# Regrouping the end of a recurrence and the products around its group norm, in a two-layer decoder step

## The reference, cut to what matters

```python
def step(s, inp):                     # one token of the recurrence; s is the state of each head, 64 x 64
    r_t, w_t, k_t, v_t, kk_t, kka_t = inp
    sa = einsum('bhvk,bhk->bhv', s, -kk_t)
    s = s * w_t[:, :, None, :] + sa[..., None] * kka_t[:, :, None, :] + v_t[..., None] * k_t[:, :, None, :]
    return s, einsum('bhvk,bhk->bhv', s, r_t)
...
mu = mean(y, -1); var = mean(square(y - mu), -1)          # over each head's 64 channels
y = ((y - mu) * rsqrt(var + GN_EPS)) * lnx_g + lnx_b
y = (y + bonus) * g                                       # g: the gate, sigmoid(gd) @ gate_up
...
out = concat([ya, yb], -1) @ w_out                        # ya from the recurrence, yb from the gMLP gate
```

## Time and profile before

| | |
|---|---|
| median of 3 runs | 1141.65 us (1141.34 to 1144.91) |
| profiled execution: its own time | 1145.79 us |
| profiled execution: span, first to last instruction | 1144.0 us |
| mean granted TensorE clock in it | 0.961 of full |
| busy: TensorE matmul | 1076.3 us |
| busy: VectorE | 804.7 us |
| busy: ScalarE | 640.1 us |
| DMA | 271.07 MB, mean 237 GB/s |

### The profile page before, as it was taken

How to read it: one execution, slowest core, us unless ns; L and a number is a source line. 1 busy time by engine, 2 the same in 40 slices (tenths; PEclk the granted TensorE clock), 3 DMA queues, 4 the chain that set the end, 5 groups by cost and what they waited for, 6 DMA issues and landing times.

```text
span 1144.0 us, 17555 instructions
## 1 busy us (share of the span) xinstructions
PE 1076.3 (94%) x7410; PEld 899.2 (79%) x7410; DVE 804.7 (70%) x901; ACT 640.1 (56%) x652; POOL 16.2 (1%) x23
## 2 busy tenths in 40 slices
PE   8999999999999999999967988889999999999996
PEld 8999889877688888888856956568768888888884
DVE  5358545475778989989852676374578898988983
ACT  4556223433666777777742332464367777777672
POOL 0000000000000000000003000000000000000000
PEclk9989999699999999999987989989999999999998
DMA  9332100225479999999926478562458999999961
GB/s 345 122 112 81 39 3 3 75 100 200 185 287 355 351 351 351 361 358 350 359 90 249 148 272 313 204 254 97 162 216 312 353 350 346 361 360 357 357 241 48
DMA packets 40324, 271.07 MB, mean 237 GB/s; under 512 B 5056, under 2 KB 5520, under 8 KB 9520
## 3 DMA queue, kind: packets, MB, share of 16 engines
q1 hardware_dynamic: 39616, 267.11, 63.2%
q0 software_dynamic: 624, 2.76, 0.6%
HBM read 265.78 MB, written 4.07 MB: 236 GB/s over the span
## 4 chain that ended last, share of the span: by engine, by line
PE 84%; DVE 6%; ACT 3%; DMA 3%; issue 3%; SPq 0%; DVEq 0%; ACTq 0%
PE ps L908 10%; PE ps L909 10%; PE ps L910 10%; PE ps L934 5%; PE ps L936 5%; PE ps L935 5%; PE ps L355 4%; PE ps L356 4%; PE ps L357 4%; PE ps L1716 3%; DMA arena<-in_k_near 3%; PE ps L946 1%; PE ps L921 1%; PE ps L947 1%; ACT w_hi L340 1%
## 5 line engine op out<-in xcount | busy, mean ns | idle before, releaser
L347 DVE TENSOR_TENSOR w_lo<-raw,w_hi 128x2048 fp32r<-128x2048 f32 x76 | 174.0, 2289 | 46.8 <-ACT w_hi L340 46.8
L340 ACT ACTIVATE w_hi<-raw 128x2048 fp32r<-128x2048 f32 x76 | 145.4, 1914 | 93.8 <-PE ps L357 38.0
L347 DVE TENSOR_TENSOR lo_more<-raw_more,hi_more 128x2048 fp32r<-128x2048 f32 x48 | 109.9, 2289 | 20.6 <-ACT hi_more L340 20.6
L347 DVE TENSOR_TENSOR w_lo<-raw_more,w_hi 128x2048 fp32r<-128x2048 f32 x48 | 109.9, 2290 | 15.6 <-ACT w_hi L340 15.5
L347 DVE TENSOR_TENSOR lo_more<-raw,hi_more 128x2048 fp32r<-128x2048 f32 x48 | 109.9, 2290 | 15.3 <-ACT hi_more L340 15.3
L340 ACT ACTIVATE hi_more<-raw 128x2048 fp32r<-128x2048 f32 x48 | 91.9, 1915 | 27.6 <-PE ps L910 27.6
L355 PE MATMUL ps<-h_hi,w_hi 128*128 128x320 f32 x320 | 103.2, 323 | 0.0
L340 ACT ACTIVATE w_hi<-raw_more 128x2048 fp32r<-128x2048 f32 x48 | 92.0, 1917 | 16.8 <-PE ps L936 16.8
L356 PE MATMUL ps<-h_lo,w_hi 128*128 128x320 f32 x320 | 101.0, 316 | 0.0
L357 PE MATMUL ps<-h_hi,w_lo 128*128 128x320 f32 x320 | 100.6, 314 | 0.0
L340 ACT ACTIVATE hi_more<-raw_more 128x2048 fp32r<-128x2048 f32 x48 | 91.9, 1914 | 11.4 <-PE ps L936 10.0
(11 more groups left out here) (502 smaller groups left out, 2335.4 us busy)
## 6 DMA issues: line engine op xcount, KB each, us to landing
raw<-in_stream SPq DMA_DIRECT2D x125, 1024.0 KB, 7.0
raw_more<-in_stream SPq DMA_DIRECT2D x96, 1024.0 KB, 7.1
arena<-in_k_near SPq DMA_DIRECT2D x8, 1024.0 KB, 9.5
arena<-in_v_near SPq DMA_DIRECT2D x8, 1024.0 KB, 7.5
arena<-in_k_far SPq DMA_DIRECT2D x8, 512.0 KB, 5.2
arena<-in_v_far SPq DMA_DIRECT2D x8, 512.0 KB, 5.0
arena<-in_bias_prompt SPq DMA_DIRECT2D x1, 1536.0 KB, 7.7
xt<-in_x SPq DMA_DIRECT2D x2, 640.0 KB, 4.8
```

What stands on the lines that cost most here:

```text
L340: eng.activation(hi_slot(W_SLOT[c]), raw_chunk(c), ACT.Copy).then_inc(S("w_hi_made"), 1)
L347: eng.tensor_tensor(lo_slot(W_SLOT[c]), raw_chunk(c), hi_slot(W_SLOT[c]), ALU.subtract).then_inc(S("w_lo_made"), 1)
```

## The change

It moves work within the engines' lists and adds four filler matmuls; nothing is computed differently. On VectorE the sample chunk's `add(2, 2)` goes ahead of `step(3)`, and `split_lo(AT_OUT0)` goes behind `y_add(4, 2)`. On TensorE four fillers of 128x256 go between `chunk_rest(4, 2)` and the wait for `y_made`. The output products of row tiles 4 to 7 are regrouped: tiles 0 and 1 whole (24 matmuls) ahead of the sum of squares (18 before), tile 2 whole (12) between that and the spread (12 before, of tiles 1 and 2), and half of tile 3 (6) between the spread and the gate (12 before, of tiles 2 and 3). The six matmuls after the gate stay.

```diff
             wkv_pe(eng)
+            for _ in range(4):
+                eng.matmul(ps[:, 1, 256:512], h_hi[:, 0, 0:P], h_hi[:, 0, 0:256], start=True, stop=True)
             eng.wait_ge(S("y_made"), 5)
...
             out0_rows(eng, 0, (4, 5, 6, 7), True, False)
-            out0_rows(eng, 1, (4, 5), True, False)
+            out0_rows(eng, 1, (4, 5, 6, 7), True, False)
             eng.wait_ge(S("mix0_vector"), MIX0_VECTOR["gn_centred"])
             eng.wait_ge(S("gn_sq"), 1)
             head_sums(eng, 0, s5).then_inc(S("gn_sums"), 1)
-            out0_rows(eng, 1, (6, 7), False, False)
-            out0_rows(eng, 2, (4, 5), True, False)
+            out0_rows(eng, 2, (4, 5, 6, 7), True, False)
             eng.wait_ge(S("mix0_vector"), MIX0_VECTOR["gn_turned"])
             for j in range(HT):
                 head_spread(eng, j, j, gn_rinv).then_inc(S("gn_spread"), 1)
-            out0_rows(eng, 2, (6, 7), False, False)
             out0_rows(eng, 3, (4, 5), True, False)
...
             eng.tensor_tensor(gu, gu, sbias, ALU.mult).then_inc(S("mix0_vector"), 1)
+            add(2, 2)
             step(3)
-            add(2, 2)
             y_add(3)
...
             eng.tensor_tensor(out, add_, ps[0:TS, 0, :].rearrange("p (j w t) -> p w j t", j=HT, w=2), ALU.add).then_inc(S("rhs_made"), 1)
-            split_lo(eng, AT_OUT0)
             eng.wait_ge(S("q_done"), 5)
             eng.tensor_copy(SET_S.e2[0:TS].rearrange("p s t -> p (s t)"), ps[0:TS, 3, :]).then_inc(S("q_kept"), 1)
             eng.wait_ge(S("sample_as_kept"), 2)
             y_add(4, 2)
+            split_lo(eng, AT_OUT0)
```

## The result

| | before | after |
|---|---|---|
| median | 1141.3 us (1134.95 to 1147.26, 20 runs) | 1133.83 us (1129.6 to 1139.35, 20 runs) |
| ratio to before | | 0.9932, 95% interval 0.9914 to 0.9951 |
| profiled execution, span | 1144.0 us | 1133.0 us |
| mean granted clock of the profiled execution | 0.961 | 0.970 |

The change makes the kernel 7.5 us faster by the medians and 7.8 us by the ratio. The two profiled executions differ by more, 11.0 us of span; why is a question for the experiments.

The account below looks back on a forecast made before the run. TensorE, 84% of the chain that ended last, was taken to bound the kernel. 1145.79 - 8.9 - 1.1 = 1135.8 us against the profile, 1131.7 against the median, taken as 1132.8; range 1129.5 to 1140.5.

Parts of the forecast that it names:

- The gap and its cause: Ahead of `third(2)`: TensorE idles because `add(2, 2)` stands behind `step(3)` on VectorE; moving it wins 1.55 us.
- The clock as most of the gain: Up to the end of the head sums: 8.9 us won, 1.55 from the gap, the rest from full clock.
- step 4: Ahead of `chunk_solved`: `add(2, 3)` waits behind L2169 on VectorE, so `chunk_solved` starts some 0.15 us late.
- step 5: At the solution's copy: moving `split_lo(AT_OUT0)` is worth nothing at half clock, about 1 us at full clock.
- step 7: Ahead of the head sums: four new fillers in a 0.59 us gap cost nearly 0.1 us at full clock, 0.6 at half.
- The load behind the split: Load behind `split_lo(AT_OUT0)`: comes some 8 us later relative to TensorE's work, needed only far behind; costed at nothing.
- The regrouping: From the mean to `sample_adds`: net 0.5 us, with half the second low stretch 1.1 us, between 0.5 and 1.8.
- that term: Second low stretch, behind the squares' sum: 1.3 us more won if it goes; half was taken.
- The turns: Rival: the clock falls later, at the turns after `third(2)`; 1140.6 us against the profile, 1136.5 against the median; chance 0.16.
- My sum: Both stretches, from `add(2, 2)` to `sample_adds`: 8.9 and 1.1 us won, 1145.79 to 1135.8 us against the profile.
- the rival of the unprofiled executions: Rival: unprofiled executions had no such low stretch, so only 2.5 to 4 us gained, 1137.7 to 1139; chance 0.09.
- My allowance for executions without the long stretch: Whole time: a fast execution may already lack part of the low stretch, so 1132.8 us instead of 1131.7.

Follow-up runs that it names:

- experiment 1: Changed kernel with `add(2, 2)` put back behind `step(3)`, so the idle time ahead of `third(2)` returns: 1141.14 us, ratio 0.9998 to the kernel before.
- experiment 9: Changed kernel with `add(2, 2)` put back behind `step(3)` and nine fillers of 128x256 ahead of `third(2)`: 1131.98 us, ratio 0.9927 to the kernel before.
- experiment 2: Kernel before with only `add(2, 2)` moved ahead of `step(3)`: 1138.55 us, ratio 0.9976.
- experiment 6: Changed kernel with `split_lo(AT_OUT0)` put back in front of the solution's copy: 1138.56 us, ratio 0.9965 to the kernel before.
- experiment 5: Kernel before with nine fillers of 128x256 between `chunk_writes(3)` and `third(2)`, VectorE's order untouched: 1140.75 us, ratio 0.9990.
- experiment 3: Changed kernel without the four new fillers: 1132.96 us, ratio 0.9917 to the kernel before.
- execution 7: One more profiled execution of the kernel before, unchanged: 1139.40 us.
- execution 8: One more profiled execution of the changed kernel, unchanged: 1128.81 us.
- execution 11: A later profiled execution of the kernel before, unchanged: 1136.81 us.
- experiment 4: Changed kernel with the output products grouped as before (18, 12, 12 and 6 matmuls): 1134.52 us, ratio 0.9967 to the kernel before.

## Why the prediction was right

**The gap and its cause.** Right. L2089 starts as soon as the products of `second(2)` are there, and TensorE goes on from `chunk_writes(3)` to `third(2)` without a break.

**The clock as most of the gain.** Right, and shown: experiments 1 and 9 differ in nothing but whether TensorE idles ahead of `third(2)` or works on fillers, and their ratios differ by 0.7%, with `third(2)` starting 6.06 us behind `second(2)` in both. The chain from the start of `second(2)` to the mean was worked out as 14.8 us (196.05 to 210.85); it took 14.95 (198.08 to 213.03), with 8.7 us won against my 8.9. The small wait of step 4 is there, 0.07 us instead of 0.15, since TensorE came to it a little later.

**The split (step 5).** Right: nothing at half clock, 1.0 us of waiting at full clock, by experiments 2 and 6. Its further effect on the clock I didn't price; experiments 2 and 5 show the clock falling behind that wait, the profile of experiment 6 doesn't.

**The new fillers (step 7).** Their price was right: the idle time of 0.59 us gave way to 0.67 us of fillers, which put the mean 0.01 us later, and the time can't tell the two apart in experiment 3.

**The load behind the split**, costed at nothing, cost nothing: TensorE shows no new wait in the stretch, and from 240 to 330 us it waits for the same three vector operations, 2.2, 1.3 and 0.4 us, in executions 7 and 8.

**The regrouping.** I took 1.1 us between 0.5 and 1.8; the pair of profiles shows 2.2, a little above my upper end (0.5 and 1.3, with no low clock in the stretch). Step by step: the squares' sum starts 3.6 us behind the mean's start, and 3.2 before; the gate starts 4.5 us behind the spread's, and 5.5 before. At like clock the regrouping itself is worth 0.7 us, against my 0.5: 17.06 us from the mean to `sample_adds` in execution 11, which has no low clock there, against 16.38, and 18.53 against 17.83 in experiments 4 and 3. Whether the clock stays up behind the squares' sum is a matter of the execution: it did in both profiles of the changed kernel and in experiment 9, and fell in those of experiments 3 and 6, which have the same grouping. Taking half of that term was a guess, and the first pair of profiles happened to show it whole.

**The turns.** The rival that the clock would fall there was wrong in all eight profiles without the gap. Execution 8 has all twelve turns in this stretch (busy times):

```profile
200.60:211.00 10.40, 10.21 (x129) 8.62 (x124) 7.38 (x9) 8.94 (x11) 0.54 (x1) 1.00 0.05 15
```

The Trainium skill (TensorE: Matmul & The Clock Gate, Part 4: PE-mode transpose) says that transposes don't count as busy for the clock the way other matmuls do. These turns took 1.4 us between other matmuls, and nothing of it showed; a longer run of turns wasn't tried.

**From 10.0 to 7.5 us.** My sum, 10.0 us, fits one execution with the long stretch against one without: the first pair of profiles differs by 11.0 us of span, executions 7 and 8 by 10.6 us of time. The median gain is smaller because the timed runs of before don't all have it, the rival of the unprofiled executions in part. Execution 11 gives that rival's price, 3.9 us, where I had 2.5 to 4.

The clocks of the timed runs agree. The 20 of the changed kernel have a mean clock of 0.9718, 64 us of low clock in 1134; those of before in the first four experiments (30 runs) have 0.9671, 75 us. That is 11 us less low clock on average, where the first pair of profiles had 20 us less in the changed stretch (17.0 and 3.3 in the earlier trace rows, none after). A straight line through these 30 runs gives 0.49 us of time for each us of low clock, so 11 us are worth about 5.4. With the 1.55 of the gap and the 0.5 of the regrouping as I had priced them, that makes 7.4, against 7.5 measured. This sum is an estimate made after the result, and two of its terms were never timed by themselves. It agrees with the result and doesn't prove it.

My allowance for executions without the long stretch was the step from 1131.7 to 1132.8, 1.1 us, and it was too small: the sum came out 2.5 us above the median gain. (The other 3.0 us between 1135.8 and 1132.8 are the offset of the profiled execution from the median, 4.1, less this allowance.) So I forecast 8.85 us of gain and 7.5 were measured; the median of before was also 0.35 us lower in 20 runs than in 3, and 1132.8 stands against 1133.83.

What stays open is what decides, in one execution of before, between 17 us of low clock and 3.

## What to carry to other kernels

A short idle time of TensorE in front of thin, serial matmuls can cost many times its length: 8.6 us for 1.39 between the profiles of experiments 1 and 9. These matmuls need not bring the clock back: in four of the five profiles with the gap it stayed low for 13.6 to 17 us. So look for the granted clock behind each gap before the gap itself is priced. Prices read inside a low stretch hide other waits: a vector operation that looks covered there can stand on the path once the clock is up, so the chain must be rebuilt with prices at full clock. And where an order can't be mended, matmuls that nobody reads, as many as fill the gap, can do in its place: here the timing didn't tell them from the better order, though the trace has them 1.7 us later. In the kernel before, where the next idle time stayed, neither the fillers nor the better order alone showed a gain clear of the noise.

## What the runs showed of the hardware

The same kernel on the same chip varies by 1.3% from one execution to the next (1133.02 to 1147.40 us in 30 runs of before), and most of it goes with the mean granted clock, 0.974 in the first and 0.963 in the last of these (correlation of time and low clock 0.95). I had expected the low stretches to be a property of the program. In four profiled executions of one program, the stretch behind the same 1.39 us of idle time lasted 17, 17, 13.6 and 3.3 us. One profiled execution is then a draw: its low stretches are to be checked in a second and a third before their whole length is put into a sum.
